# Two attentions, the product behind each, and the query transposes of one product group: moved work and removed matmul bursts in a two-block transformer kernel

## The reference, cut to what matters

```python
# layer 1 of the first block
q, k, v = jnp.split(x @ w_in, 3, axis=-1)
q = partial_rope(heads(q), cos, sin) * (DL_HEAD_DIM ** -0.5)
k = partial_rope(heads(k), cos, sin)
...
return o.transpose(0, 2, 1, 3).reshape(B, S, D) @ w_out      # od_w_out
...
# second block
z = h @ w_in[l]
q, k, v, su, sv, ga, gb = jnp.split(z, splits, axis=-1)
...
y_att = gqa_attention(q, k, v) @ w_att_out[l]
merged = jax.nn.sigmoid(ga) * y_att + jax.nn.sigmoid(gb) * y_sgu
```

## Time and profile before

| | us |
|---|---|
| median of 3 runs | 2353.04 (2352.3 to 2356.09) |
| the profiled execution | 2353.56 |
| its span, first to last instruction | 2351.7 |
| mean granted TensorE clock | 0.979 |
| TensorE busy | 2226.4 (95% of the span) |
| VectorE busy | 1301.9 (55%) |
| ScalarE busy | 1110.2 (47%) |

### The profile page before, as it was taken

One profiled execution on the slowest core, in us unless ns is written; L12 is line 12 of the kernel. 1 busy time (PEld: TensorE's weight loads), 2 busy tenths in 40 slices (PEclk: granted clock), 3 DMA queues, 4 the chain that ended last, 5 costly groups with the idle time before them and its releaser, 6 DMA issues.

```text
span 2351.7 us, 30074 instructions
## 1 busy us (share of the span) xinstructions
PE 2226.4 (95%) x11002; PEld 1816.3 (77%) x11002; DVE 1301.9 (55%) x1916; ACT 1110.2 (47%) x1648; POOL 54.6 (2%) x70
## 2 busy tenths in 40 slices
PE   6999999999999999999999999999999679999994
PEld 5877788888888876788888888867888468888883
DVE  3456663333374346553333467642554469988996
ACT  3435453423432237363432444473344258888884
POOL 1000000000000000000000000000000010000001
PEclk8999999999999999999999999999999879999997
DMA  5221233323323320233323333303222199999995
GB/s 168 94 72 37 72 108 99 98 89 101 96 74 106 90 72 1 81 126 99 97 92 97 99 99 103 90 10 99 84 90 78 58 347 411 408 411 409 406 403 186
DMA packets 129139, 338.60 MB, mean 144 GB/s; under 512 B 10528, under 2 KB 11712, under 8 KB 129040
## 3 DMA queue, kind: packets, MB, share of 16 engines
q1 hardware_dynamic: 117744, 296.85, 36.3%
q0 software_dynamic: 7840, 27.59, 3.4%
q10 hardware_dynamic: 3456, 12.81, 1.3%
HBM read 320.96 MB, written 16.25 MB: 143 GB/s over the span
## 4 chain that ended last, share of the span: by engine, by line
PE 87%; DVE 7%; ACT 3%; DMA 1%; issue 1%; SPq 0%; POOL 0%; DVEq 0%; ACTq 0%; POOLq 0%
PE bank L2236 41%; PE bank L2239 18%; PE bank L2633 11%; PE bank L2670 5%; PE bank L2317 2%; PE bank L2326 2%; PE bank L2387 1%; PE bank L2260 1%; DVE w_l L1327 1%; PE bank L2613 1%; PE bank L2341 1%; DMA w_raw<-in_ev_w_in_dram 1%; ACT w_h L809 1%; DVE xt_l L1394 1%; ACT arena L830 1%
## 5 line engine op out<-in xcount | busy, mean ns | idle before, releaser
L1327 DVE TENSOR_TENSOR w_l<-w_raw,w_h 128x1024 fp32r<-128x1024 f32 x370 | 447.6, 1222 | 592.1 <-ACT w_h L809 588.7
L809 ACT CAST w_h<-w_raw 128x1024 fp32r<-128x1024 f32 x370 | 386.3, 1052 | 738.7 <-PE bank L2236 512.9
L2236 PE MATMUL bank<-w_h,xt_h 128*128 128x512 f32 (+1 forms) x960 | 377.5, 393 | 13.3 <-issue 6.1
L2236 PE MATMUL bank<-w_h,xt_l 128*128 128x512 f32 (+1 forms) x960 | 372.6, 388 | 0.0
L2236 PE MATMUL bank<-w_l,xt_h 128*128 128x512 f32 (+1 forms) x960 | 372.2, 388 | 0.0
L2239 PE MATMUL bank<-xt_h,w_h 128*128 128x512 f32 x608 | 237.6, 391 | 11.1 <-DVE xt_l L1349 8.8
L2236 PE MATMUL bank<-w_h,ht_h 128*128 128x512 f32 x624 | 244.0, 391 | 0.7 <-DVE w_l L1327 0.7
L1327 DVE TENSOR_TENSOR w_l<-spare,w_h 128x1024 fp32r<-128x1024 f32 x184 | 220.6, 1220 | 41.6 <-ACT w_h L809 41.0
L2236 PE MATMUL bank<-w_h,ht_l 128*128 128x512 f32 x624 | 242.9, 389 | 0.0
L2236 PE MATMUL bank<-w_l,ht_h 128*128 128x512 f32 x624 | 242.8, 389 | 0.0
L2239 PE MATMUL bank<-xt_h,w_l 128*128 128x512 f32 x608 | 237.1, 390 | 0.0
(11 more groups left out here) (355 smaller groups left out, 2924.5 us busy)
## 6 DMA issues: line engine op xcount, KB each, us to landing
w_raw<-in_ffn_w_dram SPq DMA_DIRECT2D x128, 512.0 KB, 3.7
spare<-in_w_down_dram SPq DMA_DIRECT2D x92, 512.0 KB, 6.6
spare<-in_w_gate_dram SPq DMA_DIRECT2D x88, 512.0 KB, 7.2
w_raw<-in_w_up_dram SPq DMA_DIRECT2D x88, 512.0 KB, 6.3
w_raw<-in_w_in_dram SPq DMA_DIRECT2D x30, 512.0 KB, 3.7
w_raw<-in_ev_w_in_dram SPq DMA_DIRECT2D x28, 512.0 KB, 3.6
w_raw<-in_od_w_in_dram SPq DMA_DIRECT2D x24, 512.0 KB, 3.7
slot_y_dram<-slot_out ACTq DMA_DIRECT2D x23, 512.0 KB, 6.8
```

The source lines that it names most:

```text
L809: nc.scalar.copy(w_h[:, n % SLOTS, :], raw_of(n)).then_inc(sem("w_hi"), 1)
L1327: V.tensor_tensor(w_l[:, s_, :], raw_of(n), w_h[:, s_, :].bitcast(F32), ALU.subtract)\
L2236: mm = T.matmul(bank[set0 + m][:, 0:g.width], a[:, c, toks_of(m)], b[:, kk, :], start=first, stop=last)
```

## The change

It does four things. The three calls of `keep_busy` and the function go. In `m1` the query transposes of product k-1 are issued inside product k, behind bank 2 of piece 2, and the wait for ScalarE's copies stands at the product's end. `pairs` gets a `follower`, the product group behind it, and issues the follower's piece 0 at k = n, that is behind transposes n-2 and values n-3 and ahead of the last step's transposes and the last two steps' values; it waits there for the last reading of the score banks and for `chunks` head pairs of `ot_lo` (6 in `dilated`, none in `gqa`). The wait for all of `ot_lo` moves behind piece 2 of `out0` in `dilated`, and behind the whole group `m2_gates[1]` in `gqa`. So that the piece finds free banks, `out0` of layer 1 now uses banks 0 to 3, and `out1` and `proj` use 4 to 7.

```diff
         tail1 = tail_groups(1, t["od_w_out"][0], NQ * HID)
+
+        tail1[0][0].set0, tail1[0][1].set0 = 0, 4
+        for g in tail1[2]:
+            g.set0 = tail1[0][1].set0
...
-            def keep_busy(g, n, spare):
-
-
-                pe.wait_ge(sem("w_lo"), g.n + 1)
-                w = w_h[:, g.n % SLOTS, 0:HALF]
-                for _ in range(n):
-                    T.matmul(bank[spare][:, :], w[:, 0:P], w, start=True, stop=True)
...
-                    if k == 3 and warm is not None:
-                        keep_busy(warm, 16, O_BANK)
...
-            def pairs(name, steps, probs, pt, work, warm):
+            def pairs(name, steps, probs, pt, work, chunks, follower):
...
-                    if k == 3:
-                        keep_busy(warm, 16, B_BANK)
...
                         mm.then_inc(sem("at_spread"), 1)
-
+                    if k == n:
+
+                        pe.wait_ge(sem("at_prob" if steps[0].mask is None else "at_max"), 2 * (s0 + n))
+                        pe.wait_ge(sem("ot_lo"), ot.start[name] + chunks)
+                        product(follower, js=(0,))
                 pe.wait_ge(sem("at_out"), s0 + n)
-                pe.wait_ge(sem("ot_lo"), ot.start[name] + ot_chunks[name])
...
-                    product(outp[0], js=(0, 1, 2))
+                    product(outp[0], js=(1, 2))
 
                 transpose(f"p{layer}", tiles_of(PTOK), waits=[[(sem("p_in"), 16 * (layer + 1))]] * NT)
+                if layer:
+                    pe.wait_ge(sem("ot_lo"), ot.start["dilated"] + ot_chunks["dilated"])
                 product(outp[0], js=(3,))
...
-                if k:
+                if 1 <= k <= 4:
+                    product(g, then={(2, 2): lambda k=k: query_chunks(f"qk{k - 1}", tiles_of(l_stage), 4)})
+                    copied(f"qk{k - 1}", 4)
+                elif k:
                     product(g)
-                if 1 <= k <= 4:
-                    query_chunks(f"qk{k - 1}", tiles_of(l_stage), 4)
-                    copied(f"qk{k - 1}", 4)
             all_free(seq[-1].g)
-            pairs("dilated", dilated_steps, l_probs, l_pt, l_work, tail1[0][0])
+            pairs("dilated", dilated_steps, l_probs, l_pt, l_work, 6, tail1[0][0])
...
-            pairs("gqa", gqa_steps, g_probs, g_pt, g_work, m2_gates[1])
+            pairs("gqa", gqa_steps, g_probs, g_pt, g_work, 0, m2_gates[1])
+            product(m2_gates[1], js=(1, 2, 3))
+            pe.wait_ge(sem("ot_lo"), ot.start["gqa"] + ot_chunks["gqa"])
...
-            for g in (*m2_gates[1:], *m2_att, m2_sgu[0]):
+            for g in (*m2_gates[2:], *m2_att, m2_sgu[0]):
```

More of the change, by code:

```diff
@@ L2327, in trans, with attention @@
                 mm.then_inc(sem("at_trans"), 1)
-            def attention(name, steps, probs, pt, ot_src=None, warm=None, extra=None):
+            def attention(name, steps, probs, pt, ot_src=None, extra=None):
                 s0, n = un.start[name], len(steps)
@@ L2490, in hgrn_transposed @@
                     mm.then_inc(sem("tr_done"), 1)
-            attention("diff", diff_steps, d_probs, d_pt, warm=tail0[0][0], extra=hgrn_transposed)
+            attention("diff", diff_steps, d_probs, d_pt, extra=hgrn_transposed)
             tail(0, tail0)
```

## The result

The changed kernel takes 2333.73 us in the median of four runs (2329.62 to 2334.83), the kernel before 2353.28 on the same chip: a ratio of 0.9912, 95% interval 0.9895 to 0.9929, that is 20 us less (17 to 25). Measured again later beside other kernels it took 2331.9 against 2354.15 (0.9904, 0.9889 to 0.9919), 22 us less. The forecast was 2330, the range 2326.5 to 2338. The profiled execution is the slowest of the first four, 2334.83 us with a span of 2333.0.

A forecast was written before the change was run, and what follows sets the result against it. TensorE's own queue was taken as the bound. Bursts 10.1, seams 4.4 and attention ends 4.5 and 4.1 sum to 23.1 us off the profiled 2353.56: 2330.5, or 2330.0 for the median; range 2326.5 to 2338.

The forecast's parts named there:

- burst in `diff`: Removing the 16 `keep_busy` matmuls in `diff` gains 3.0 us (bounds 1.5 and 3.77), VectorE becoming last in steps 3 to 5.
- burst in `dilated`: Removing the 16 `keep_busy` matmuls ahead of step 1's transposes in `dilated` gains 3.3 us (bounds 2.5 and 3.76).
- burst in `gqa`: Removing the 16 `keep_busy` matmuls in `gqa` gains the full 3.76 us (bounds 3.0 and 3.76).
- four seams: Issuing `m1`'s query transposes inside the next product hides ScalarE's copies at four product boundaries: 4.4 us, bounds 0 and 4.8.
- end of `dilated`: Issuing the next product's first piece before `dilated`'s last transposes gains 4.5 us, of which 1.9 is the clock.
- end of `gqa`: Issuing the next product's first piece before `gqa`'s last transposes gains 4.1 us, of which 1.9 is the clock.
- the wait for ScalarE of 0.4 us in `dilated`: In `dilated`, one TensorE wait for ScalarE (4.3/8 = 0.5 us a head) comes back without the burst, lowering 3.76 to 3.3.
- the half-hidden rival: In the attentions, ScalarE or VectorE run ahead during the bursts, so half of 10.1 us is lost: 2335 us; chance 10%.
- the cover of 2 us: In `m1`, ScalarE's query copies finish some 2 us before the product ends, hidden under its last 30 matmuls.
- Rival 1: The clock still dips behind `dilated`, `gqa` or both: 1.9 us each, 2333.8 us if both; chance 18%.
- Rival 4: The bursts held TensorE's clock; without them it falls to half in the attentions, up to some 2494 us; chance 3%.
- The prediction's 26 us: In the three attentions, 26 us at the low clock level was given as the point from which lost clock decides.

## Why the prediction was right, point by point

| term | forecast | measured by stages |
|---|---|---|
| burst in `diff` | 3.0 | 3.4 (54.86 - 51.46), 3.7 with a dip on both sides |
| burst in `dilated` | 3.3 | 3.7 |
| burst in `gqa` | 3.76 | 3.6 |
| four seams | 4.4 | 4.5 |
| end of `dilated` | 4.5 | 4.2 (2.6 and the clock 1.6) |
| end of `gqa` | 4.1 | 3.6 (both with its dip) |
| sum | 23.1 | 23.0 |

**The sum** held to 0.1 us as a sum, in part by luck: the bursts were forecast 0.6 us too low and the ends 0.8 too high. It also counts the dip behind `dilated` whole, and the old end had it in 3 of 5 profiled executions only; at that share the dip is worth 1.0 us and the sum 22.4, an estimate from these five.

**The bursts.** Right that they lay on the path whole. The deductions that I made by hand were too large: the wait for ScalarE of 0.4 us in `dilated` did not come back, and of the burst in `diff` 0.2 to 0.3 us came back and not 0.7; that it was VectorE was only argued, as the new pauses are too short for the trace to name what ended them. That the half-hidden rival is wrong was shown by the two kernels without and with double bursts.

**The seams.** Right in size and in mechanism; the cover of 2 us that was worked out for the copies is what the trace shows. Both halves of the difference were taken 0.1 us too small and cancel: 16 transposes inside the product cost 1.75 us and not 1.64, and the old seam 24.67 - 21.79 = 2.88 and not 2.75.

**The ends.** The mechanism was right, the clock's share mis-sized: I took 1.9 us a dip, it measured 1.6. The start of the second piece of the old end was read off a cast's release (962.75), which comes some 0.2 us behind the last matmul's issue; the transposes of `p` at 973.46 less two pieces give 962.5. That one misreading made both the dip and the gain of the end too large, in `dilated` and in `gqa`. The rest of the 0.5 us at `gqa` was not followed up. Rival 1 did not come: the clock fell behind no new end. The prediction had named the shorter pause and the dense piece before it beside each other; the kernel with the piece outside, in its one profiled execution, held the clock with the shorter pause alone. The swap of the bank sets, put at zero, cost nothing that the stages show: from `p` to `gqa` it is 559.33 us with it and 559.34 without.

**Where the median stayed behind the sum.** 20 and 22 us where 23 were forecast, and 23 lies inside both intervals (17 to 25, 19 to 26), so the gap is not clear of noise. One step the prediction did not take all the same: I treated the clock's dips as fixed places of the profiled execution, to be removed or kept, and took the rest of the kernel as a block. Apart from the old end of `gqa`, which had one in 5 of 5, they come and go. Each other candidate place (one or two pauses of TensorE of 0.7 to 2.4 us) has one in some executions and not in others, the same program included: at the start of `diff` in 4 of 6 profiled executions of kernels with its burst and in 6 of 7 without, in `sv` in 4 of 11 with its pause, behind `cross` in 6 of 11 with its old end. The kernel before happened to be profiled in one without a dip at the start of `diff`. The profiled execution of the changed kernel accounts for itself: 23.0 by the stages, less 1.3 (dip in `diff`), 1.6 (dip in `sv`) and 1.2 (the later rise of the clock in the first product) is 18.9; the profiled executions differ by 2353.56 - 2334.83 = 18.7. That this luck also makes the difference of the medians was only argued. The rise in the first product is the largest such term: the first scores of `diff` start at 208.15 to 211.44 us in the 13 profiled executions, though nothing before them differs. Why `sv` had no dip in any of five executions with the old ends and had four in six with the new ones and the pause is open; by chance alone four dips in eleven would fall so in one case of 22 (an estimate from these counts).

**Rival 4**, that the bursts hold the clock, is wrong: in all eight executions without their bursts `dilated` and `gqa` run at 1.00 up to their ends, and at the start of `diff`, where the clock does fall, it falls before the burst in all four of the executions that have both. The prediction's 26 us for the point from which this rival decides do not follow from its own terms: at half of the clock, 23 us of matmul work would eat the 23.1. The Trainium skill, TensorE: Matmul & The Clock Gate, Part 1, says that the window in which the clock gate watches TensorE runs freely and doesn't reset when the kernel starts, so that the moment of a change of level differs from run to run. The runs agree: same program, dips in other places. By that rule a single profiled execution can't say which dips a change will remove.

## What to carry to other kernels

Work that is only there to keep an engine busy costs its full issue time where that engine is the bound; look whether the clock falls before it, as then it can hold nothing. Whether such work in the pause itself would hold the clock was not tried. Shorten the pause at the end of a sparse stage with work that does not depend on its last result, and move each wait to the first instruction that needs it: at `dilated` the later wait brought 1.2 us, and 1.6 more where the clock would have dipped, the earlier piece 1.3. When a profile shows dips of the clock, price them, but forecast them as chances over several executions, not as rows.

## What the runs showed of the hardware

- Behind the old ends (a pause of 2.31 us after a sparse tail) the granted clock fell in 3 of 5 profiled executions at `dilated` and in 5 of 5 at `gqa`; behind a pause of 0.89 us or none in 0 of 8 and 0 of 8. I had expected the dense piece ahead of the pause to matter; in the one execution without it the clock held at both ends too.
- A dip cost 1.6 us in `dilated`, in `sv` and in `diff` with its burst, and 1.0 to 1.3 in `diff` without. At the start of `diff` it came behind two pauses of 1.06 and 1.43 us, in 10 of 13 profiled executions.
- The times of one program, the kernel before, spread from 2350.05 to 2357.77 us in 21 runs; what makes that spread was not shown; its profiled executions (2353.56 and 2353.78) differ by 0.2 us, with dips in partly other places.
